# The state chain of a scan half in one step, halves five steps apart and eleven long

## The chip, the cores and the metric

The program runs on one NeuronCore of a Trainium2 chip. The metric is the device time of one execution, in microseconds (us); the median of several runs counts.

## What is computed

Two transformer blocks, one behind the other, with all weights in HBM. The first, one layer over 512 tokens, mixes dilated attention, a gated linear attention (GLA) and block attention. The second, two layers over 512 tokens and 256 context tokens, mixes a Fourier part, attention and a recurrent scan that runs forward and backward. Both scans are chunked forms of the same recurrence. In short:

```python
def step(s, inp):                      # one chunk
    cum = jnp.cumsum(lf, axis=2)       # log forget gates, summed in the chunk
    last = cum[:, :, -1:, :]
    s_new = jnp.exp(last[:, :, 0, :])[..., None] * s + \
        jnp.einsum('bhsd,bhse->bhde', kc * jnp.exp(last - cum), vc)
    o_inter = jnp.einsum('bhtd,bhde->bhte', qc * jnp.exp(cum), s)
    decay = jnp.exp(jnp.where(mask, diff, -jnp.inf))
    att = jnp.einsum('bhtd,bhsd,bhtsd->bhts', qc, kc, decay)
    return s_new, o_inter + jnp.einsum('bhts,bhse->bhte', att, vc)
```

The result is the same whatever the chunk. Every chunk's state needs the state of the chunk before: s_new = decay * s + update.

## The kernel before

The projections and feed-forward products take most of the time: each fp32 product is made of three passes of rounded high and low parts (`gemm_pe`, lines 655 and 658). Between the projections of a layer lie three **scan stages**, one for each layer. I call them stage G (first block, the GLA scan beside causal attention, 245 to 392 us of the trace), stage M (second block, layer 0, 1100.0 to 1260.2) and stage N (layer 1, 2129.5 to 2286.3). Ahead of and behind them lie projections.

In a scan stage every engine runs two programs that the function `branch` interleaves: the scan and "the other", the attention (and in M and N the Fourier part behind it). Each is a generator that yields its position between 0 and 1 after each step; `branch` always takes the one that is behind. So the order of instructions on each engine is fixed when the program is built: it follows from the number of steps of either side, not from times. All engines use the same positions. An engine runs its instructions strictly in this order, and waits at semaphores.

**Attention step** (`att_pe`, `att_act`, `att_dve`, `att_pool`; "step 6" is its number): TensorE makes scores against one block of 128 keys for two heads (line 1052, then a shift, 1064), ScalarE takes exponentials (1234), TensorE multiplies the exponentials of the step before with the values (1085). GpSimd adds exponentials up (1190). At the end of a group of heads come column sums on TensorE (1102), the reciprocal on ScalarE (1241, 1243) and the weighting on VectorE (1161). Scores of two heads fill two banks, so TensorE can begin step s+1 only when the first exponential of step s is done. The products with the values of a new group wait until the reciprocal of the group before last has been begun (`taken`), and the sums of a group wait for the weighting of the group before (`weighted`). Stage M has 32 such steps, 24 with 512 columns and 8 with 256; N has 24; the causal G has 24, and there each score also waits for a maximum that VectorE takes (1141).

**Scan half** (`scan_pe`, `scan_act`, `scan_dve`; n = 0 to 3): M and N have four halves, two of the forward and two of the backward scan; G has one. A half goes through steps k:
- k=0: floor of the gate on VectorE (1356), exponentials and logarithms on ScalarE (1512, 1515, 1520, in layer 1 also 1524)
- k=1: the cumulative sum (1368 or 1370); k=2: differences (1381 to 1386), then the decay and two exponentials on ScalarE (1529 to 1534)
- k=3: q and k scaled (1391, 1393); k=4: differences (1398, 1400), one exponential (1538); k=5: 1405 to 1411, two exponentials (1541, 1544)
- k=6: q and k for the state (1417, 1421); TensorE makes the scores inside the chunks (1605 to 1614)
- k=7: masks (1432); TensorE transposes the keys (1622); ScalarE copies them (`k_tok`, 1549)
- k=8: TensorE makes the **updates** of all chunks (1631) into PS2 and PS3; VectorE begins the **chain**, one instruction for a link (1450)
- k=9: second part of the chain; k=10: TensorE makes the **outputs** (1644 from the scores, 1650 from the states), which wait for the whole chain
- k=11: VectorE copies the outputs out (1462 or 1464)

Half n begins LAG turns behind half n-1, so in one turn step k of a half meets step k-6 of the next:

```python
LAG = 6
SCAN_TICKS = 12
for tick in range(ticks):
    for n in reversed(range(len(hs))):      # VectorE: the later half first
        if 0 <= tick - LAG * n < SCAN_TICKS:
            step(n, tick - LAG * n)
    yield (tick + 1) / (ticks + READ_TICKS)
```

TensorE and ScalarE take the earlier half first. With H halves there are (H-1) * LAG + SCAN_TICKS turns, 30 for four halves and 12 for one, and five more turns that read the result out. A half's chain has 23 links in M and N (24 chunks of 32 tokens), 15 in G.

Of the kernel before, what the change touches and what calls it, by code (L numbers as in the profile page):

```python
# [46 lines left out]
EXP_CAP = 85.0  # L47
SUB = 16
CH = 32
LAG = 6  # L50


COLS = {}
# [83 lines left out]
def blocks_kernel(nc, dram, out_t):  # L137
# [24 lines left out]
    with ExitStack() as ctx:  # L162
# [166 lines left out]
        v_step = sem("dve_step")  # L329
# [999 lines left out]
        def bank(i):  # L1329
            return PS[2 + i // 2][:, 512 * (i % 2):512 * (i % 2) + 512]  # L1330

        SCAN_TICKS = 12
        READ_TICKS = 5

        def scan_ticks(ss):
            n = sum(s.H for s in ss)
            return (n - 1) * LAG + SCAN_TICKS

# [3 lines left out]
        def scan_dve(v, st, ss):  # L1342
            S = lambda n: local(st, n)
# [3 lines left out]
            def step(n, k):  # L1347
                s, u = hs[n]
# [73 lines left out]
                if k == 7:  # L1422
# [6 lines left out]
                    m = masks[:, int(s.back), :].unsqueeze(1).to_broadcast([P, s.n_out, CH])  # L1429
                    for r in range(s.R):  # L1430
# [2 lines left out]
                                                  blocks(bank(r)[:, 0:w], CH)).then_inc(tell.sem, 1)  # L1433
                        if tell is v_step:
                            v_step.up()
                if k in (8, 9):
                    states = blocks(s.room["states"][:], HD)
                    links = list(zip(s.chain, s.chain[1:]))
                    if k == 8:
                        if n >= 1:  # L1440
                            v.wait_ge(S("outputs").sem, S("outputs").at(n))
                        nc.vector.memset(states[:, s.chain[0], :], 0.0).then_inc(v_step.sem, 1)
                        v.wait_ge(v_step.sem, v_step.up())
                        v.wait_ge(S("decay").sem, S("decay").at(n + 1))
                        v.wait_ge(S("updates").sem, S("updates").at(n + 1))
                    m = -(-len(links) // 2)
                    for i in range((k - 8) * m, min(len(links), (k - 7) * m)):
                        a_, b_ = links[i]
                        tell = S("states") if i == len(links) - 1 else v_step
                        nc.vector.scalar_tensor_tensor(states[:, b_, :], states[:, a_, :], s.room[f"decay{n % 2}"][:, a_:a_ + 1],  # L1450
                                                       bank(a_ % 4)[:, a_ // 4 * HD:a_ // 4 * HD + HD], ALU.mult, ALU.add).then_inc(tell.sem, 1)
                        if tell is v_step:
                            v.wait_ge(v_step.sem, v_step.up())
                if k == 11:
                    v.wait_ge(S("outputs").sem, S("outputs").at(n + 1))
                    for w in range(s.R // 2):
                        dst = s.out(u + w)[:, 0:s.own].rearrange("p (t j c) -> p j t c", j=4, c=CH)
                        for j in range(4):
                            tell = S("out") if w == s.R // 2 - 1 and j == 3 else v_step
                            src = blocks(bank(j)[:, w * s.own // 4:(w + 1) * s.own // 4], CH)  # L1460
                            if s.back:
                                nc.vector.tensor_tensor(dst[:, j], src, dst[:, j], ALU.add).then_inc(tell.sem, 1)
                            else:
                                nc.vector.tensor_copy(dst[:, j], src).then_inc(tell.sem, 1)
                            if tell is v_step:
                                v_step.up()
# [7 lines left out]
            s = ss[-1]  # L1474
# [104 lines left out]
        def scan_pe(p, st, ss):  # L1579
            S = lambda n: local(st, n)  # L1580
# [3 lines left out]
            def step(n, k):  # L1584
                s, u = hs[n]
# [38 lines left out]
                if k == 8:  # L1624
# [7 lines left out]
                                              room["k_tok"][rows, P * t + s.dk * r:P * t + s.dk * r + s.dk],  # L1632
                                              s.v(t, s.R * u + r)[rows, :], start=True, stop=True)
                    mm.then_inc(S("updates").sem, 1)
                if k == 10:
                    p.wait_ge(S("states").sem, S("states").at(n + 1))
                    states = blocks(room["states"][:], HD)
                    att, qi = s.att(), s.parity("qi", n)
# [34 lines left out]
            s = ss[-1]  # L1673
# [546 lines left out]
```

## Time and profile before

| | us |
|---|---|
| median of 3 runs | 2752.66 |
| lowest, highest run | 2739.95, 2752.67 |
| profiled execution, its own time | 2748.97 |
| profiled execution, its span | 2746.8 |
| TensorE busy | 2520.5 (92% of the span) |
| VectorE, ScalarE, GpSimd busy | 855.2, 792.6, 782.4 |
| mean granted clock of TensorE | 0.944 |
| stage M, stage N | 160.2, 156.8 |

The time of an execution is a little above the span, which goes from the first to the last instruction. A granted clock of 1.00 is 2.4 GHz, 0.50 is 1.2 GHz. An entry "[5.29 <-DVE s_states L1450]" says that the engine stood idle for 5.29 us before this row, and that what it waited for last was VectorE's line 1450. PE is TensorE, DVE VectorE, ACT ScalarE, POOL GpSimd.

### The profile page before, as it was taken

What the parts mean: (1) busy time and instruction counts of PE and PEld (TensorE: products, weight loads), DVE (VectorE), ACT (ScalarE), POOL (GpSimd) and SP (SyncE); (2) the same over time, 40 slices, a digit from 0 to 9 for tenths busy, and PEclk for the clock granted to TensorE, in tenths of its full rate; (3) what the DMA queues carried; (4) which work ended last, traced back from release to release, by engine and by line L of the source; (5) the groups of instructions that cost most, each with busy time, mean ns of one, the idle gap of its engine ahead of it and who ended that gap; (6) DMA issues with size and microseconds to landing.
All of it is one profiled execution on the core that took longest, in us unless ns stands there. A gap on an engine that the chain in (4) does not pass through costs nothing.

```text
span 2746.8 us, 38017 instructions
## 1 busy us (share of the span) xinstructions
PE 2520.5 (92%) x16714; PEld 1938.7 (71%) x16714; DVE 855.2 (31%) x1287; ACT 792.6 (29%) x1007; POOL 782.4 (28%) x262
## 2 busy tenths in 40 slices
PE   4998788999998899887989999999799877899998
PEld 3876556777776678345878888888568335688886
DVE  3002335442444541762241101102441652411113
ACT  3122233222224421543232112112431533322222
POOL 1232232333432211420222222222221331344442
PEclk9798799999999999998999999999999778999999
DMA  6542013434443110101111111111210102222221
GB/s 179 129 166 71 17 39 127 180 154 182 156 177 122 56 39 1 46 3 62 62 47 62 62 62 63 71 58 48 71 46 9 45 2 78 77 97 103 92 94 60
DMA packets 42952, 220.52 MB, mean 80 GB/s; under 512 B 4072, under 2 KB 12920, under 8 KB 19492
## 3 DMA queue, kind: packets, MB, share of 16 engines
q1 hardware_dynamic: 35624, 200.52, 20.0%
q10 hardware_dynamic: 7164, 17.57, 2.5%
q8 instruction: 132, 2.16, 0.3%
q14 instruction: 32, 0.26, 0.0%
HBM read 212.05 MB, written 6.03 MB: 79 GB/s over the span
## 4 chain that ended last, share of the span: by engine, by line
PE 75%; DVE 6%; ACT 2%; issue 1%; DMA 0%; POOL 0%; ACTq 0%; DVEq 0%; POOLq 0%
PE PS L655 59%; PE PS L658 3%; PE PS L1052 2%; PE PS L1085 2%; DVE s_states L1450 2%; DVE tmp L587 1%; PE PS L716 1%; DVE a_lo L579 1%; PE PS L1650 1%; PE PS L1758 1%; PE PS L1849 1%; PE PS L537 1%; PE PS L1102 1%; PE PS L1064 1%; PE PS L1826 0%
## 5 line engine op out<-in xcount | busy, mean ns | idle before, releaser
L1967 POOL TENSOR_TENSOR w_lo<-raw,w_hi 128x2048 fp32r<-128x2048 f32 (+2 forms) x146 | 648.6, 4442 | 1617.1 <-ACT w_hi L752 1617.1
L655 PE MATMUL PS<-a_hi,w_hi 128*128 128x512 f32 (+1 forms) x2104 | 698.2, 376 | 90.0 <-DVE a_lo L579 58.4
L655 PE MATMUL PS<-a_lo,w_hi 128*128 128x512 f32 (+1 forms) x2104 | 675.8, 366 | 0.0
L655 PE MATMUL PS<-a_hi,w_lo 128*128 128x512 f32 (+1 forms) x2104 | 673.5, 365 | 0.0
L655 PEld LDWEIGHTS PS<-a_hi,w_hi 128*128 128x128 f32 x2104 | 361.1, 191 | 185.6 <-issue 115.7
L655 PEld LDWEIGHTS PS<-a_lo,w_hi 128*128 128x128 f32 x2104 | 362.4, 191 | 65.9 <-issue 0.7
L655 PEld LDWEIGHTS PS<-a_hi,w_lo 128*128 128x128 f32 x2104 | 359.0, 190 | 66.8
L752 ACT ACTIVATE w_hi<-raw 128x2048 fp32r<-128x2048 f32 (+2 forms) x146 | 270.4, 1852 | 373.8 <-PE PS L655 185.3
L655 PE MATMUL PS<-hid_hi,w_hi 128*128 128x512 f32 (+1 forms) x784 | 262.5, 371 | 0.0
L655 PE MATMUL PS<-hid_lo,w_hi 128*128 128x512 f32 (+1 forms) x784 | 259.0, 367 | 0.0
L655 PE MATMUL PS<-hid_hi,w_lo 128*128 128x512 f32 (+1 forms) x784 | 258.5, 366 | 0.0
L866 DVE TENSOR_TENSOR tmp<-PS,sq 128x768 f32<-128x768 f32 (+1 forms) x44 | 36.3, 825 | 486.4 <-PE PS L655 486.4
L1190 POOL TENSOR_TENSOR acc<-acc,pt 128x512 f32<-128x512 f32 (+3 forms) x100 | 119.7, 1197 | 203.2 <-PE PS L1085 152.1
L655 PEld LDWEIGHTS PS<-hid_hi,w_hi 128*128 128x128 f32 x784 | 135.0, 188 | 30.8 <-issue 6.6
L804 ACT ACTIVATE hid_hi<-tmp 128x512 fp32r<-128x512 f32 (+1 forms) x76 | 52.8, 694 | 358.3 <-DVE tmp L866 250.5
L655 PEld LDWEIGHTS PS<-hid_lo,w_hi 128*128 128x128 f32 x784 | 135.6, 188 | 25.4
L655 PEld LDWEIGHTS PS<-hid_hi,w_lo 128*128 128x128 f32 x784 | 134.4, 188 | 25.5
L852 DVE SCALAR_TENSOR_TENSOR x<-PS,mods,x 128x512 f32<-128x512 f32 x64 | 48.1, 751 | 288.3 <-PE PS L655 288.2
L869 DVE TENSOR_TENSOR hid_lo<-tmp,hid_hi 128x512 fp32r<-128x512 f32 (+1 forms) x76 | 99.8, 1313 | 69.3 <-ACT hid_hi L804 69.3
L1052 PE MATMUL PS<-proj 64*128 64x512 f32 (+3 forms) x208 | 100.1, 652 | 17.2 <-ACT acc L1234 13.2
L658 PE MATMUL PS<-w_hi,a_hi 128*128 128x256 f32 (+1 forms) x352 | 103.9, 295 | 4.0 <-POOL w_lo L1967 4.0
L658 PE MATMUL PS<-w_lo,a_hi 128*128 128x256 f32 (+1 forms) x352 | 102.5, 291 | 0.0
(203 smaller groups left out, 2473.8 us busy)
## 6 DMA issues: line engine op xcount, KB each, us to landing
raw<-in_w_ada SPq DMA_DIRECT2D x48, 1024.0 KB, 6.9
raw<-in_w_ff SPq DMA_DIRECT2D x32, 1024.0 KB, 4.7
raw<-in_w_in SPq DMA_DIRECT2D x27, 1024.0 KB, 4.8
raw<-in_w_gate SPq DMA_DIRECT2D x22, 1024.0 KB, 4.7
raw<-in_w_up SPq DMA_DIRECT2D x22, 1024.0 KB, 4.7
raw<-in_w_down SPq DMA_DIRECT2D x16, 1024.0 KB, 4.7
raw<-in_w_out SPq DMA_DIRECT2D x12, 1024.0 KB, 5.8
raw<-in_w_down SPq DMA_DIRECT2D x8, 768.0 KB, 4.3
```

Source lines behind the costliest of these rows:

```text
L655: mm = p.matmul(ps[:, dst], wv[:, k, idx * P:(idx + 1) * P], av[:, k, dst], start=first, stop=last)
L658: mm = p.matmul(ps[:, 0:ncol], av[:, k, idx * P:(idx + 1) * P], wv[:, k, 0:ncol], start=first, stop=last)
L752: nc.scalar.activation(w_hi[:, m % 2, 0:kt, 0:ncol], raw[:, i % 3, 0:kt, 0:ncol], ACT.Copy).then_inc(s_hi.sem, 1)
L804: nc.scalar.activation(hid_hi[:, tile, span(parts)], tmp[:, h % 2, span(parts)], ACT.Copy).then_inc(s_hhi.sem, 1)
L852: nc.vector.scalar_tensor_tensor(dst[:, tile, own], ps[:, src], mods[:, l, o, c:c + 1], dst[:, tile, own], ALU.mult, ALU.add).then_inc(tel ...
L866: nc.vector.tensor_tensor(tmp[:, h % 2, sp_], ps[:, sp_], sq[:, tile % 2, sp_], ALU.mult).then_inc(s_relu.sem, 1)
L869: nc.vector.tensor_tensor(hid_lo[:, tile, sp_], tmp[:, h % 2, sp_], hid_hi[:, tile, sp_].bitcast(F32), ALU.subtract).then_inc(low.sem, 1)
L1052: p.matmul(turned_ps(m)[:, lo:n], hd["k"][:, P * j:P * (j + 1)], hd["q"][:, grp["c0"] + lo:grp["c0"] + n], start=True, stop=False)
L1085: mm = p.matmul(values_ps(plan, g)[hd["rows"], lo:n], hd["v"][j], exps(plan, s, h, lo, n), start=first, stop=last)
L1190: pool.tensor_tensor(total_, total_, pt[:, s % 2, h, lo:n], ALU.add).then_inc(S("added").sem, 1)
L1450: nc.vector.scalar_tensor_tensor(states[:, b_, :], states[:, a_, :], s.room[f"decay{n % 2}"][:, a_:a_ + 1], bank(a_ % 4)[:, a_ // 4 * HD:a ...
L1967: pool.tensor_tensor(w_lo[:, m % 2, 0:kt, 0:ncol], src, w_hi[:, m % 2, 0:kt, 0:ncol].bitcast(F32), ALU.subtract).then_inc(s_lo.sem, 1)
```

## The change

LAG becomes 5 and SCAN_TICKS 11. The whole chain is made in step k=8; the outputs move from k=10 to k=9 and the copies from k=11 to k=10. The number of turns falls from 30 to 26 in M and N (35 to 31 with the reading), and from 12 to 11 in G (17 to 16), so each turn is a larger share of the stage and the places of all scan steps among the attention steps shift. In one turn step k of a half now meets step k-5 of the next half, and step 10 of a half, step 5 of the next and step 0 of the one after meet.

```diff
-LAG = 6
+LAG = 5
...
-        SCAN_TICKS = 12
+        SCAN_TICKS = 11
...
-                if k in (8, 9):
+                if k == 8:
                     states = blocks(s.room["states"][:], HD)
                     links = list(zip(s.chain, s.chain[1:]))
...
-                    m = -(-len(links) // 2)
-                    for i in range((k - 8) * m, min(len(links), (k - 7) * m)):
-                        a_, b_ = links[i]
+                    for i, (a_, b_) in enumerate(links):
                         tell = S("states") if i == len(links) - 1 else v_step
                         nc.vector.scalar_tensor_tensor(states[:, b_, :], states[:, a_, :], s.room[f"decay{n % 2}"][:, a_:a_ + 1],
                                                        bank(a_ % 4)[:, a_ // 4 * HD:a_ // 4 * HD + HD], ALU.mult, ALU.add).then_inc(tell.sem, 1)
                         if tell is v_step:
                             v.wait_ge(v_step.sem, v_step.up())
-                if k == 11:
+                if k == 10:
                     v.wait_ge(S("outputs").sem, S("outputs").at(n + 1))
...
-                if k == 10:
+                if k == 9:
                     p.wait_ge(S("states").sem, S("states").at(n + 1))
```

Three lines are gone, so a line number of the scan above 1441 is three or so lower in the changed kernel.

ScalarE in stage N, where half 0's step 5 meets half 1's step 0. Before (E is the exponential's output, pt the attention's exponentials, acc those of a group's first step):

```order
602 L1234 ACTIVATE pt<-PS 128x512 x2
603 L1541 ACTIVATE s_E_113<-s_X 128x768
604 L1544 ACTIVATE s_E_114<-s_d 128x768
605 L1234 ACTIVATE pt<-PS 128x512 x2
606 L1512 ACTIVATE proj<-proj 128x768
607 L1515 ACTIVATE s_lf_pad<-proj,small 128x768
608 L1520 ACTIVATE s_F<-s_lf_pad 128x768
609 L1524 ACTIVATE s_lf_pad<-s_F,lbs 128x768
610 L1234 ACTIVATE acc_82<-PS 128x512 x2
```

and now:

```order
599 L1234 ACTIVATE pt<-PS 128x512 x2
600 L1538 ACTIVATE s_E_113<-s_X 128x768
601 L1541 ACTIVATE s_E_114<-s_d 128x768
602 L1509 ACTIVATE proj<-proj 128x768
603 L1512 ACTIVATE s_lf_pad<-proj,small 128x768
604 L1517 ACTIVATE s_F<-s_lf_pad 128x768
605 L1521 ACTIVATE s_lf_pad<-s_F,lbs 128x768
606 L1234 ACTIVATE pt<-PS 128x512 x2
607 L1234 ACTIVATE acc_82<-PS 128x512 x2
```

The exponentials of attention step 5 stood between the two groups of the scan and stand behind both now.

TensorE in stage M, half 1, from the column sums of step 18 to the outputs (the updates stood ahead of step 18 before, with four steps of one row 1052 to 1085 each between transposes and outputs). Before:

```order
4098 L1102 MATMUL PS<-acc_82,ones 64x512 x2
4099 L1102 MATMUL PS<-pt,ones 64x512 x2
4100 L1052 MATMUL PS<-proj,k_swap 128x512
4101 L1052 MATMUL PS<-proj 128x512
4102 L1064 MATMUL PS<-shift,ones_r 128x512 x2
4103 L1085 MATMUL PS<-acc_82,tok_57 64x512 x2
4104 L1052 MATMUL PS<-proj,k_swap 128x512
4105 L1052 MATMUL PS<-proj 128x512
4106 L1064 MATMUL PS<-shift,ones_r 128x512 x2
4107 L1085 MATMUL PS<-pt,tok_57 64x512 x2
4108 L1644 MATMUL PS<-s_att_128,tok_57 64x32 x48
```

and now:

```order
4097 L1102 MATMUL PS<-acc_82,ones 64x512 x2
4098 L1102 MATMUL PS<-pt,ones 64x512 x2
4099 L1628 MATMUL PS<-tok_57,s_k_tok 64x64 x48
4100 L1052 MATMUL PS<-proj,k_swap 128x512
4101 L1052 MATMUL PS<-proj 128x512
4102 L1064 MATMUL PS<-shift,ones_r 128x512 x2
4103 L1085 MATMUL PS<-acc_82,tok_57 64x512 x2
4104 L1641 MATMUL PS<-s_att_128,tok_57 64x32 x48
```

The updates (1628) have moved behind the sums, and one attention step instead of three lies between them and the outputs. In M the halves have 2, 1, 2 and 0 steps there (3, 3, 3 and 0 before), in N 1, 1, 1 and 0 (2, 2, 2 and 0 before).

VectorE in stage M, half 2. Before:

```order
493 L1442 MEMSET s_states 128x64
494 L1450 SCALAR_TENSOR_TENSOR s_states<-s_states,s_decay_126,PS 128x64 x12
495 L1161 TENSOR_TENSOR proj<-PS,inverse 128x512
496 L1391 TENSOR_TENSOR s_qb<-proj,s_E_113 128x768
497 L1393 TENSOR_TENSOR s_kb<-proj,s_E_114 128x768
498 L1450 SCALAR_TENSOR_TENSOR s_states<-s_states,s_decay_126,PS 128x64 x11
```

and now:

```order
490 L1391 TENSOR_TENSOR s_qb<-proj,s_E_113 128x768
491 L1393 TENSOR_TENSOR s_kb<-proj,s_E_114 128x768
492 L1441 MEMSET s_states 128x64
493 L1447 SCALAR_TENSOR_TENSOR s_states<-s_states,s_decay_126,PS 128x64 x23
494 L1161 TENSOR_TENSOR proj<-PS,inverse 128x512
```

Step 3 of the next half (1391, 1393) has come ahead of the chain, and the weighting (1161) has moved from behind 12 links to behind all 23.

## Rows read from the trace of the kernel before

**Rows 1.** Windows: busy time by engine and granted clock, stages M and N

```profile
core 0: us, PE busy (x) PEld busy (x) DVE busy (x) ACT busy (x) POOL busy (x), PEclk, DMA share, GB/s
1100.00:1260.20 160.20, 134.52 (x2520) 68.04 (x2520) 103.05 (x188) 68.86 (x121) 48.72 (x32) 0.87 0.06 21
2129.50:2286.30 156.80, 122.09 (x1832) 56.07 (x1832) 88.04 (x184) 64.27 (x101) 44.08 (x32) 0.76 0.06 21
```

**Rows 2.** What TensorE waited for, longest first, in stage N

```profile
PE PS L1644 <- DVE s_states L1450: 23.9, 4, 8.0
```

**Rows 3.** TensorE in time order (start, duration, what, [idle before]), N, half 0

```profile
2155.24 0.73 PE L1614 MATMUL PS<-s_qb,s_kb 64*32 64x32 f32 x62
2156.43 0.69 PE L1052 MATMUL PS<-proj 64*128 64x512 f32 x1
2160.64 0.87 PE L1622 MATMUL PS<-ident,s_ko 128*128 128x128 f32 x6
2164.01 1.25 PE L1631 MATMUL PS<-tok,s_k_tok 32*64 32x64 f32 x96
2176.35 1.18 PE L1644 MATMUL PS<-s_att,tok 32*64 32x32 f32 x64 [5.29 <-DVE s_states L1450]
```

**Rows 4.** VectorE in order of time, stage N, half 0

```profile
2165.97 3.76 DVE L1450 SCALAR_TENSOR_TENSOR s_states<-s_states,s_decay,PS 128x64 f32<-128x64 f32 x12
2169.77 0.69 DVE L1161 TENSOR_TENSOR proj<-PS,inverse 128x512 f32<-128x512 f32 x1
2171.20 1.74 DVE L1393 TENSOR_TENSOR s_kb<-proj,s_E 128x512 f32<-128x512 f32 x1
2172.86 3.43 DVE L1450 SCALAR_TENSOR_TENSOR s_states<-s_states,s_decay,PS 128x64 f32<-128x64 f32 x11
```

**Rows 5.** ScalarE in order of time, stage N, halves 0 and 1

```profile
2154.51 0.84 ACT L1544 ACTIVATE s_E<-s_d 128x768 f32<-128x768 f32 x1 [1.08 <-DVE s_d L1411]
2155.26 1.07 ACT L1234 ACTIVATE pt<-PS 128x512 f32<-128x512 f32 x2
2156.21 0.84 ACT L1512 ACTIVATE proj<-proj 128x768 f32<-128x768 f32 x1
2157.09 0.94 ACT L1515 ACTIVATE s_lf_pad<-proj,small 128x768 f32<-128x768 f32 x1
2158.06 0.84 ACT L1520 ACTIVATE s_F<-s_lf_pad 128x768 f32<-128x768 f32 x1
2158.93 1.03 ACT L1524 ACTIVATE s_lf_pad<-s_F,lbs 128x768 f32<-128x768 f32 x1
2161.55 0.81 ACT L1549 ACTIVATE s_k_tok<-PS 128x768 f32<-128x768 f32 x1 [0.61 <-PE PS L1622]
```

**Rows 6.** TensorE in order of time, stage M, half 1

```profile
1168.78 0.88 PE L1622 MATMUL PS<-ident,s_ko 128*128 128x128 f32 x6
1172.09 1.25 PE L1631 MATMUL PS<-tok,s_k_tok 32*64 32x64 f32 x96
1183.06 1.17 PE L1644 MATMUL PS<-s_att,tok 32*64 32x32 f32 x96
```

**Rows 7.** TensorE in order of time, stage M, half 2

```profile
1210.10 0.65 PE L1085 MATMUL PS<-acc,tok 128*64 128x256 f32 x4 [0.53 <-ACT inverse L1241]
1216.62 1.12 PE L1102 MATMUL PS<-acc,ones 128*64 128x256 f32 x4 [3.15 <-DVE proj L1161]
```

**Rows 8.** Windows: the 11 us behind half 0's wait in stage N

```profile
2176.30:2187.30 11.00, 10.95 (x142) 6.12 (x142) 5.08 (x12) 3.39 (x5) 2.54 (x2) 0.50 0.01 1
```

**Rows 9.** TensorE in time order: products with the states, M, halves 0 and 3

```profile
1153.41 2.99 PE L1650 MATMUL PS<-s_qi,s_states 64*64 64x32 f32 x96
...
1254.97 5.33 PE L1650 MATMUL PS<-s_qi,s_states 64*64 64x32 f32 x96
```

**Rows 10.** VectorE in order of time, stage G

```profile
323.44 2.50 DVE L1450 SCALAR_TENSOR_TENSOR s_states<-s_states,s_decay,PS 128x64 f32<-128x64 f32 x8 [2.19 <-PE PS L1631]
```

**Rows 11.** TensorE in order of time, stage G

```profile
326.32 0.39 PE L1039 MATMUL PS<-a_lo,a_hi 64*128 64x256 f32 x1 [0.16 <-DVE small L1141]
```

More of the change, by code:

```diff
@@ L1435, in step @@
                             v_step.up()
-                if k in (8, 9):
+                if k == 8:
                     states = blocks(s.room["states"][:], HD)
                     links = list(zip(s.chain, s.chain[1:]))
[L1439 to L1445, printed above, removed]
-                    m = -(-len(links) // 2)
-                    for i in range((k - 8) * m, min(len(links), (k - 7) * m)):
-                        a_, b_ = links[i]
+                    if n >= 1:
+                        v.wait_ge(S("outputs").sem, S("outputs").at(n))
+                    nc.vector.memset(states[:, s.chain[0], :], 0.0).then_inc(v_step.sem, 1)
+                    v.wait_ge(v_step.sem, v_step.up())
+                    v.wait_ge(S("decay").sem, S("decay").at(n + 1))
+                    v.wait_ge(S("updates").sem, S("updates").at(n + 1))
+                    for i, (a_, b_) in enumerate(links):
                         tell = S("states") if i == len(links) - 1 else v_step
```

## The prediction

> **What bounds the kernel now.** I read the windows of the stages first, then the waits of TensorE, then the timelines around the state chain. TensorE is the engine that sets the end nearly everywhere; in the scan stages it is not full. In stage M it is busy 134.5 of 160.2 us at a mean granted clock of 0.87, in stage N 122.1 of 156.8 us at 0.76 [rows 1]. So a stage gets longer when TensorE waits more or when its clock stays low longer; its work is the same before and after. In stage N the largest wait is four times the same one: the outputs of a half (line 1644) wait for the state chain on VectorE, 23.9 us in all, 8.0 the longest [rows 2]. Rows 3 and 4 show one of these. The updates end at 2164.01 + 1.25 = 2165.26. Then TensorE has two attention steps, about 2.9 us each, and stands 5.29 us until 2176.35 [rows 3]. VectorE meanwhile runs chain (3.76), the attention's weighting (0.69), the next half's step 3 (about 2.4 us between 2170.46 and 2172.86) and chain (3.43) [rows 4]. These 11.1 us are what the change wants to shorten.
>
> **What moves.** Nothing is removed: the 23 links of a half stay 23 links, 3.76 + 3.43 = 7.2 us [rows 4]. What changes is which work lies between two waits.
> (a) VectorE: the chain runs in one piece behind the updates, and the next half's step 3 comes ahead of it.
> (b) TensorE: between updates and outputs lie now one or two attention steps where two or three were.
> (c) ScalarE: a half's step 5 and the next half's step 0 now fall in one turn, and so do step 7 and the next half's step 2. The exponentials of the attention step are queued behind the pair. TensorE can begin the next attention step without them, but not the one after.
>
> **Stage N, cost of each part.**
> Outputs' wait. Path behind the updates: about 0.15 to the first link, 7.2 of chain, 0.1 to TensorE, together 7.45, less one step of 2.9: 4.6 in place of 5.29, a gain of 0.7 in halves 0 to 2. In half 3 the weighting (0.69) no longer lies between the two pieces: 0.7 too. Together -2.8.
> Given back: step 3 of the next half must end before the chain starts. It needs that half's two exponentials, which now stand behind k_tok. Counted from the transposes: k_tok ends at 2162.36 - 2160.64 = 1.7 [rows 3, 5], two exponentials of 0.84 make 3.4, step 3 makes 5.8. The updates end 4.6 behind the transposes where one step lies between [rows 3]. So 1.2 each for halves 0 and 1: +2.4. In half 2 two steps lie between, and there the attention's reciprocal stands behind the same two exponentials: +1.6. Net of the outputs' part: +1.2.
> The pair on ScalarE. Half 0's last exponential ends at 2155.35; half 1's four operations take 2156.21 to 2159.96, 3.75 us [rows 5]. Before, attention step 5 had its exponentials between the two (2155.26, 1.07 for two). Now they come after: first one ready at 2155.35 + 3.75 + 0.55 = 2159.65. TensorE is done with step 5 at 2155.24 and used to go on with scores and step 6 [rows 3]; now step 6 comes first and waits: 4.4 us. Once only, since in the later halves the products with the states (4.8 us) and the scores lie where they cover the pair.
> The clock. Behind the wait of 5.29 the granted clock is 0.50 for 11 us, the 1.2 GHz level [rows 8]. All but 0.05 us of them is busy, so at most 5.5 us is lost. A new wait of 4.4 costs between 0 and 5.5; I take 4.5, since it is nearest in length to this row.
> Stage N: 1.2 + 4.4 + 4.5 = +10.1.
>
> **Stage M.** Here three attention steps lay between updates and outputs and the wait was near nothing.
> Half 0: the reciprocal for step 7 stands behind the pair, about 1.8 us of waiting; two steps with sums almost cover the chain, 0.5. +2.3.
> Half 1: the pair is half 1's two exponentials (1.6) and three operations (2.65). With the first attention exponential it takes 4.8 us against one step of 2.8: 2.0. The exponentials behind k_tok: 0.5. Between updates and outputs one step of 2.7 is left where steps and sums filled 1172.09 + 1.25 to 1183.06 without a gap [rows 6]: 7.45 - 2.7 = 4.8. After it the clock: the 96 products on the states took 2.99 at the full clock and 5.33 at the low one [rows 9], +2.3, those on the scores +0.4, one attention step +1.8: 4.6, with bounds 0 and 5.5. Together +11.9.
> Half 2: the reciprocal waits for two more exponentials, +1.9 on the 0.53 there [rows 7]. The column sums wait for the weighting, which stood behind the first half of the chain (3.15 us [rows 7]) and stands behind all of it now: +3.4, the second piece's length [rows 4]. Clock +1.0. Together +6.3.
> Half 3: the last attention step moves into the wait for k_tok (0.9) and 0.35 of weighting leaves the chain: -1.3.
> Stage M: 2.3 + 11.9 + 6.3 - 1.3 = +19.2.
>
> **Stage G.** One half of 15 links: 8 take 2.50 [rows 10], so 4.7 in one piece. The attention there needs a maximum from VectorE for each score; one waits 0.16 now [rows 11]. It would find VectorE in the chain until 0.7 + 4.7 + 0.6 = 6.0 behind the updates, with 2.5 us of work for TensorE: 3.4. Some of it may be won back where the transposes stand one attention step later. +2, bounds 0 and 3.4.
>
> **Sum.** 10.1 + 19.2 + 2.0 = +31.3 on the profiled execution's 2748.97: 2780. The runs' median is 2752.66, 3.7 above that execution, and one run had 2739.95, so the base is known to about that.
>
> The price of a link deserves a second look: 3.43 / 11 = 0.312 us for 64 columns. [...]
>
> **Rivals.**
> 1. *The cover holds.* The pairs on ScalarE may cost nothing if its exponentials run early enough, and new waits may leave the clock alone. Then 10.6 us of pair terms and 10.1 of clock go, and +10.6 is left: 2760, within 0.5%. For it: ScalarE is busy only 69 of 160 us [rows 1]. Against: the pair is 5.4 us in one piece and TensorE is one step ahead at most. 0.20.
> 2. *Faster: the outputs' waits in stage N get short enough for the clock to stay up.* The three of 5.29 become 4.6 by the chain's path. The point from which it decides: if 4.6 us of idling leaves TensorE at 2.4 GHz and 5.29 doesn't, stage N wins 3 x 5 us of low clock, and 2.8 of waiting; with the pairs covered too, 2749 - 18 = 2731. Against: 3.15 us of waiting [rows 7] stands in a stretch whose work is already slower. 0.06.
> 3. *Every pair stalls.* If the products and scores don't cover the pairs in halves 1 and 2 either, 4.4 + 4.5 come on top perhaps twice more: 2798. 0.12.
> 4. *Nothing moves:* excluded by the order of the rows on all three engines.
>
> **How the numbers follow.** A measurement of this kernel can tell 0.5% (13.8 us) from no change. Forecast as summed: 0.62, its own range 2765 (clock terms at 0, small terms low) to 2793 (5.5 of clock behind four new waits). Rival 1: 0.20, rival 2: 0.06, rival 3: 0.12. So slower by over 0.5% (above 2766.4) 0.74, within 0.5% 0.20, faster 0.06. The range leaves out rival 2 and the low part of rival 1, and takes in rival 3: 2756 to 2800.
>
> **What would show it.** Right: in stage N one new wait of 4 to 5 us on ScalarE's exponentials near attention step 6, with the clock at 0.5 behind it; outputs' waits of 4 to 6 us; in stage M a wait of about 5 us at half 1's outputs and one of about 6.5 us for the weighting in half 2; stage M near 179 us, stage N near 167. Wrong: stage M under 170 us, no wait on exponentials, or the loss outside the three scan stages.

## The result, and the profile after

The changed kernel takes 2796.57 us (median of 4 runs, 2794.3 to 2799.63), the kernel before 2752.66 in the same comparison: ratio 1.0174, 95% interval 1.0147 to 1.0201. The medians are 43.9 us apart; the ratio stands for 48 us. The forecast was 2780, slower, with 2756 to 2800 as its range. Sign and range held; the size did not: 31 us were forecast, 44 to 48 came.

The profiled execution has 2794.3 us, span 2792.5. The windows of stages M and N, whole, as in [rows 1] (columns: from:to, length, busy time by engine, granted clock, DMA share, GB/s):

```profile
1094.94:1291.03 196.09, 157.77 (x2520) 77.48 (x2521) 97.78 (x188) 68.51 (x121) 47.15 (x32) 0.73 0.05 17
2160.31:2331.40 171.09, 134.60 (x1832) 58.91 (x1832) 81.97 (x184) 64.25 (x101) 43.48 (x32) 0.68 0.05 19
```

M went from 160.2 to 196.1 us (179 forecast), N from 156.8 to 171.1 (167 forecast). TensorE has the same instructions and is busy 23 and 12.5 us longer, at a lower clock. What TensorE waited for, in M and then in N (total us, times, longest):

```profile
PE PS L1641 <- DVE s_states L1447: 14.4, 3, 7.4
PE PS L1102 <- DVE proj L1161: 5.3, 1, 5.3
PE PS L1085 <- ACT inverse L1241: 3.7, 2, 2.1
PE PS L1052 <- ACT pt L1234: 1.8, 2, 1.4
...
PE PS L1641 <- DVE s_states L1447: 22.1, 4, 7.4
PE PS L1052 <- ACT pt L1234: 3.0, 1, 3.0
PE PS L1085 <- ACT inverse L1241: 1.6, 1, 1.6
```

In N the outputs' waits fell from 23.9 [rows 2] to 22.1, and one wait for the exponentials came new, as forecast. In M the waits for the states are 2.07, 4.94 and 7.44 us (halves 0, 1 and 3). The forecast rows in TensorE's timeline, M and then N:

```profile
1157.29 1.17 PE L1641 MATMUL PS<-s_att,tok 32*64 32x32 f32 x96 [2.07 <-DVE s_states L1447]
1232.94 0.65 PE L1085 MATMUL PS<-acc,tok 128*64 128x256 f32 x4 [2.11 <-ACT inverse L1241]
1242.96 1.12 PE L1102 MATMUL PS<-acc,ones 128*64 128x256 f32 x4 [5.32 <-DVE proj L1161]
2190.89 1.22 PE L1052 MATMUL PS<-proj 64*128 64x512 f32 x1 [3.02 <-ACT pt L1234]
2213.98 1.18 PE L1641 MATMUL PS<-s_att,tok 32*64 32x32 f32 x64 [4.98 <-DVE s_states L1447]
```

And the whole chain of a half on VectorE, 7.25 us for 23 links, the 3.76 + 3.43 of [rows 4] in one piece:

```profile
2206.68 7.25 DVE L1447 SCALAR_TENSOR_TENSOR s_states<-s_states,s_decay,PS 128x64 f32<-128x64 f32 x23
```

So the waits are those that were forecast. The clock is not. The first of these windows lies just ahead of the 2.07 us wait and the second behind it, the third behind a wait of 1.42 us, the fourth behind the 4.94 us wait:

```profile
1144.50:1154.50 10.00, 10.00 (x133) 3.97 (x134) 7.00 (x18) 5.53 (x10) 4.96 (x4) 1.00 0.01 2
1157.29:1168.49 11.20, 11.20 (x204) 7.04 (x206) 5.37 (x12) 4.69 (x8) 0.85 (x1) 0.59 0.01 3
1183.40:1191.86 8.46, 8.45 (x124) 3.34 (x124) 3.52 (x11) 3.36 (x7) 0.00 (x0) 1.00 0.01 2
1196.80:1214.00 17.20, 17.20 (x220) 9.73 (x222) 4.91 (x11) 4.92 (x8) 4.70 (x4) 0.60 0.01 2
```

TensorE was busy without a gap at the full clock, stood idle for 2.07 us, and then had a mean clock of 0.59 for 11.2 us: with the two levels 1.0 and 0.5 that is 2 x 0.41 x 11.2 = 9.2 us at 1.2 GHz, a loss of 4.6 us behind a wait of 2.07. The forecast had put waiting, and no clock, on this place. The third row begins behind a wait of 1.42 us, and there the clock stayed at 1.00. The second profile (after_again, below) has the same three waits with 0.58, 1.00 and a low clock behind them.

In half 2 the forecast had "Clock +1.0". From the column sums, which waited for the weighting, to the end of the half's outputs, before (behind 3.15 us) and after (behind 5.32 us):

```profile
1216.62:1227.37 10.75, 10.75 (x230) 7.19 (x230) 7.84 (x19) 3.65 (x9) 0.00 (x0) 0.86 0.01 2
1242.96:1254.46 11.50, 11.50 (x212) 8.60 (x212) 3.20 (x6) 2.19 (x5) 0.00 (x0) 0.50 0.00 1
```

At 0.50 the 11.50 us lose half their length, 5.75 us; at 0.86 the 10.75 us lose 1.5. So the clock cost over 4 us more here than before, against the 1.0 forecast; the second profiles of both kernels have 0.50 and 0.85.

### The profile page after: what moved, and what is told of

It reads as the page before. It is cut to its first block, busy times and chain, and to the rows that moved or that the text cites. A ratio compares the mean times of both kernels' runs of the same rounds, so it can differ in the third digit from the quotient of the medians.

```text
span 2792.5 us, 38011 instructions
## 1 busy us (share of the span) xinstructions
PE 2553.1 (91%) x16714; PEld 1950.7 (70%) x16714; DVE 843.9 (30%) x1287; ACT 792.4 (28%) x1007; POOL 779.6 (28%) x262
## 4 chain that ended last, share of the span: by engine, by line
PE 76%; DVE 6%; ACT 3%; issue 1%; POOL 0%; DMA 0%; ACTq 0%; DVEq 0%; POOLq 0%
PE PS L655 58%; PE PS L658 2%; PE PS L1052 2%; PE PS L1085 2%; DVE s_states L1447 2%; DVE tmp L587 1%; PE PS L716 1%; DVE a_lo L579 1%; PE PS L1647 1%; PE PS L1755 1%; PE PS L1846 1%; PE PS L1064 1%; PE PS L1102 1%; PE PS L537 1%; PE PS L1747 1%
## 5 line engine op out<-in xcount | busy, mean ns | idle before, releaser
L1052 PE MATMUL PS<-proj 64*128 64x512 f32 (+3 forms) x208 | 114.4, 726 | 21.4 <-ACT acc L1234 15.0
```

What stands on the lines that cost most here:

```text
L1052: p.matmul(turned_ps(m)[:, lo:n], hd["k"][:, P * j:P * (j + 1)], hd["q"][:, grp["c0"] + lo:grp["c0"] + n], start=True, stop=False)
```

## The experiments

All ratios are against runs of the kernel before on the same chip. "Spacing" is LAG, "length" is SCAN_TICKS. First the results together, ordered by what they share:

| kernel | spacing, length, chain | median us | ratio (95%) |
|---|---|---|---|
| before_again | 6, 12, split | 2750.29 | 1.0012 (0.9988 to 1.0035) |
| lag6_one12 | 6, 12, whole | 2746.93 | 0.9978 (0.9951 to 1.0005) |
| lag6_one | 6, 11, whole | 2766.90 | 1.0058 (1.0035 to 1.0082) |
| lag5_split | 5, 12, split | 2779.57 | 1.0097 (1.0066 to 1.0128) |
| lag5_one12 | 5, 12, whole | 2779.00 | 1.0078 (1.0049 to 1.0107) |
| after_again | 5, 11, whole | 2794.76 | 1.0176 (1.0133 to 1.0218) |
| lag7_one12 | 7, 12, whole | 2789.59 | 1.0138 (1.0114 to 1.0163) |
| act_k0_late | 5, 11, whole | 2795.54 | 1.0181 (1.0139 to 1.0224) |
| before_pair | 6, 12, split | 2755.07 | 1.0016 (0.9995 to 1.0037) |
| before_nochain | 6, 12, none | 2697.33 | 0.9801 (0.9758 to 0.9844) |
| pair_nochain | 6, 12, none | 2704.99 | 0.9838 (0.9804 to 0.9873) |
| after_nochain | 5, 11, none | 2719.23 | 0.9882 (0.9855 to 0.9910) |
| start_before | 6, 12, split, filled | 2756.66 | 1.0006 (0.9984 to 1.0027) |
| warm_before | 6, 12, split, filled | 2736.91 | 0.9940 (0.9916 to 0.9964) |
| warm_12 | 6, 12, whole, filled | 2738.96 | 0.9953 (0.9923 to 0.9983) |
| warm_all | 6, 12, whole, filled | 2746.78 | 0.9977 (0.9956 to 0.9998) |
| warm_after | 5, 11, whole, filled | 2788.28 | 1.0129 (1.0098 to 1.0161) |
| after_fill | 5, 11, whole, filled | 2778.44 | 1.0120 (1.0094 to 1.0147) |

### Both kernels once more

> The changed kernel unaltered, for a second profile. In the first, stage M's part up to the first outputs took 62.9 us against 52.9 before, with the same instructions and nearly the same waits, at a granted clock of 0.78 against 0.90. Theory A1 (how long the clock stays low behind the start wait of 4.3 us differs from execution to execution): that part may come out between 52 and 63 us in this profile. Theory A2 (it follows from the order of the work): 62 to 63 us again. The ratio to the kernel before stays 1.015 to 1.020.

> The kernel before unaltered, for a second profile. A1: stage M's part up to the first outputs (52.9 us, clock 0.90) may come out as long as 61 us, and stage M up to 10 us longer than 160.8 us without any edit; A2: 52 to 54 us again. Ratio 0.998 to 1.002.

The windows from the end of the attention's start wait (4.3 us in M, 5.2 in N) to the end of the last outputs, M and N, of the first and second profile before, then of the first and second after:

```profile
1107.11:1260.24 153.13, 132.97 (x2515) 67.60 (x2515) 97.45 (x182) 64.31 (x116) 48.72 (x32) 0.88 0.05 20
2136.49:2286.32 149.83, 120.48 (x1826) 55.55 (x1826) 84.47 (x180) 58.68 (x95) 44.08 (x32) 0.75 0.05 19
```

```profile
1103.60:1263.68 160.08, 139.82 (x2515) 69.13 (x2515) 94.61 (x182) 64.27 (x116) 46.64 (x32) 0.82 0.05 19
2139.73:2293.56 153.83, 124.65 (x1826) 56.39 (x1826) 83.42 (x180) 58.76 (x95) 44.21 (x32) 0.72 0.05 18
```

```profile
1102.09:1291.03 188.94, 156.14 (x2514) 77.00 (x2515) 92.14 (x182) 63.96 (x116) 47.15 (x32) 0.73 0.04 15
2167.27:2331.41 164.14, 132.98 (x1827) 58.43 (x1827) 78.42 (x180) 58.67 (x95) 43.48 (x32) 0.68 0.05 18
```

```profile
1116.51:1299.29 182.78, 150.58 (x2515) 76.60 (x2515) 94.15 (x182) 63.91 (x116) 47.70 (x32) 0.77 0.04 16
2174.66:2333.56 158.90, 123.61 (x1827) 56.34 (x1827) 81.56 (x180) 58.98 (x95) 43.68 (x32) 0.75 0.05 18
```

A1 holds in its main point: the same kernel's stage M differs by 7 us from profile to profile, all of it busy time at another clock (idle is 20.2 and 20.3). Only the place guessed was wrong: the kernel before's part up to the first outputs stayed near 53 us, and most of the difference (40.2 against 45.3 us) lies between the outputs of half 1 and those of half 2. A single pair of profiles therefore overstates or understates the clock. The means of the two are used from here; taken pair by pair, the added busy time is 10.8 to 23.2 us in M and -1.0 to 12.5 us in N. After less before: M +29.3 (busy +17.0, idle +12.3), N +9.7 (busy +5.7, idle +4.0), ahead of M +3.9, the rest +0.5. Together 43.4, which is the difference of the mean spans (2793.55 - 2750.25).

### The change taken apart: spacing, length, chain

lag6_one, against the changed kernel:

```diff
-LAG = 5
+LAG = 6
```

> Eleven steps with the whole chain in step 8, but the halves six steps apart again, so that no two halves meet on ScalarE in one tick. Theory A (the chain's path of 7.45 us now has one attention step for cover instead of two or three, and each wait that this makes on TensorE lowers its granted clock, which costs more than the wait): the time is that of the changed kernel, 2790 to 2800 us, with waits of 4.5 to 5 us in stage N. Theory B (the five-step spacing does it: two halves' exponentials meet on ScalarE): the time goes back to 2750 to 2760 us.

lag5_split, against the kernel before:

```diff
-LAG = 6
+LAG = 5
```

> Only the spacing is changed, six steps to five; the chain stays in two pieces over twelve steps. Theory A: the outputs keep two or three attention steps of cover, so no wait is added; the time is 2750 to 2762 us, and the granted clock of stages M and N stays near 0.87 and 0.76. Theory B: the waits for ScalarE's pt are there (2 to 4 us each) and the clock falls behind them, 2775 to 2800 us.

lag6_one12, against the changed kernel, first the copies, then the outputs (lag5_one12 is the same with LAG = 5):

```diff
-LAG = 5
+LAG = 6
-        SCAN_TICKS = 11
+        SCAN_TICKS = 12
-                if k == 10:
+                if k == 11:
...
-                if k == 9:
+                if k == 10:
```

> Six steps apart and twelve long as before, only the chain goes whole into step 8, the outputs stay in step 10. Theory A: the waits in front of the outputs in stage N fall from 5.3 us to 7.45 - 5.8 = 1.6 us, the clock falls less behind them, 2730 to 2745 us. Theory C (the whole chain on VectorE holds up what stands behind it, above all the weighting of an attention group, and that is where the loss comes from): new waits for VectorE of 3 to 6 us, 2760 to 2785 us.

> Five steps apart, twelve long, whole chain in step 8, outputs in step 10: the missing corner between the split chain at five apart (1.010) and the changed kernel (1.018). If the spacing and the outputs' step add up as they did at six apart (0.998 with the outputs in step 10, 1.006 in step 9): 1.006 to 1.011. If at five apart the whole chain itself is what costs, through VectorE's later weighting and copies: 1.013 to 1.018.

Neither A nor B alone: lag6_one lies between the two forecasts, lag5_split in B's range, lag6_one12 just above A's, and lag5_one12 where it was expected if the parts add up. The six kernels (these four, before and after_again) add up. Whole in place of split chain: -0.19% at five apart, -0.22% at six, which is within the uncertainty. Outputs and copies one step earlier, a half eleven steps long: +0.80% at six apart, +0.98% at five (22 and 27 us). Spacing five in place of six: +0.97%, +1.00% and +1.18% (27 to 32 us). So the change is two losses of similar size, and the piece it is named for, the chain in one step, is the one whose cost can't be told from nothing.

The waits show how. TensorE in N of lag6_one12, and then of lag6_one:

```profile
PE PS L1641 <- DVE s_states L1447: 14.0, 4, 7.4
```

```profile
PE PS L1641 <- DVE s_states L1447: 22.8, 4, 7.4
```

With one more attention step under the chain the waits of halves 0 to 2 are 2.2 us each (1.6 expected) instead of 4.94 to 5.51. Theory C's wait is seen in M: the weighting behind the whole chain is waited for 6.5 us (3.15 in [rows 7]); its loss is not seen in the time. In lag5_split a conflict comes that the changed kernel does not have, since at five apart and twelve long the copies of a half share a turn with the next half's scores. M, and then N:

```profile
PE PS L1614 <- DVE proj L1464: 7.4, 1, 7.4
...
PE PS L1085 <- ACT inverse L1241: 4.7, 3, 1.6
PE PS L1052 <- ACT pt L1234: 3.0, 1, 3.0
PE PS L1614 <- DVE proj L1464: 2.6, 1, 2.6
```

So its 1.0097 is not the price of the spacing alone; the pair lag6_one and after_again, without that conflict, gives 1.18%.

lag7_one12, against lag6_one12:

```diff
-LAG = 6
+LAG = 7
```

> Seven steps apart, twelve long, whole chain in step 8, outputs in step 10 (at six apart this measured 0.998). Theory A and D (spacing sets how much attention lies beside each half, and so the waits): the three meetings of step 6, 7 with the next half's step 0 are apart, the waits of half 0 to 2 stay at 2.2 us, but the scan ends three steps later, so that its last half has less attention beside it: 0.995 to 1.003.

A miss: 1.0138. In M:

```profile
PE PS L1085 <- ACT inverse L1241: 10.7, 4, 6.3
PE PS L1052 <- ACT pt L1234: 8.1, 3, 7.5
```

ScalarE has work in steps 0, 2, 4, 5 and 7 of a half. At six apart no two of these fall in one turn. At five, 5 meets 0 and 7 meets 2; at seven, 7 meets 0. But it is not this meeting that makes the two longest waits, of 7.51 and 6.33 us. VectorE and ScalarE ahead of the 7.51:

```profile
1133.21 7.25 DVE L1447 SCALAR_TENSOR_TENSOR s_states<-s_states,s_decay,PS 128x64 f32<-128x64 f32 x23
1142.88 0.84 ACT L1529 ACTIVATE s_E<-s_d 128x768 f32<-128x768 f32 x1 [7.90 <-DVE s_d L1386]
```

At seven apart step 8 of a half shares its turn with step 1 of the next, so the next half's step 2 (its differences, up to line 1386) stands behind the whole chain on VectorE. ScalarE stands 7.90 us for it, and the attention's exponentials are queued behind; the 6.33 comes the same way, behind 7.06 us on ScalarE. At six apart step 2 shares the turn of step 8 and VectorE takes the later half first, so it stands ahead of the chain. Wider is no better than closer: what stands behind the long chain decides here.

### Is it the meeting on ScalarE?

act_k0_late, against the changed kernel, on ScalarE:

```diff
-                if k == 0:
+                if k == (0 if n == 0 else 1):
```

> The changed kernel, but ScalarE issues step 0 of halves 1 to 3 one tick later, where the half ahead has nothing for it: no two halves meet on ScalarE. Theory B (about half of the loss is these meetings, each a wait for pt of 1.4 to 3 us and the clock behind it): those waits go and 8 to 15 us come back, ratio 1.011 to 1.014. Theory A alone (the outputs' waits do it): within 4 us of the changed kernel, ratio 1.016 to 1.019; a wait of VectorE for the logarithm, 1.5 us each, could take its place.

Nothing came back (1.0181 against 1.0176), but the test is not clean. In M and N the later step made VectorE late, and TensorE waited for that instead, and N still has a first attention wait of 3.0 us:

```profile
PE PS L1619 <- DVE s_ko L1421: 4.0, 1, 4.0
...
PE PS L1052 <- ACT pt L1234: 3.7, 3, 3.0
PE PS L1628 <- DVE s_att L1432: 2.6, 2, 1.5
```

That wait is not the meeting's: its exponentials came 19.6 us behind the end of the start wait, against 23.6 and 23.2 in the two profiles of the changed kernel, but TensorE had the higher clock and was there sooner. For the same reason the meeting's wait is 3.02 us in one profile of the changed kernel and 6.09 in the other: ScalarE is ready at the same time, and TensorE arrives 20.6 or 17.2 us behind the start wait.

The other way round is cleaner: make the meeting of 5 and 0 where there was none.

before_pair, against the kernel before, on ScalarE; VectorE makes the floor of halves 1 to 3 one turn earlier too:

```diff
-                if k == 0:
+                if k == (0 if n == 0 else -1):
...
-                    if 0 <= tick - LAG * n < SCAN_TICKS:
+                    if -1 <= tick - LAG * n < SCAN_TICKS:
```

> The kernel before, six apart, twelve long, split chain; only step 0 of halves 1 to 3 (the floor on VectorE, the exponentials and logarithms on ScalarE) is issued one tick earlier, so that it meets step 5 of the half ahead on ScalarE as it does at five apart. Theory B (the meeting itself delays pt and the reciprocals, and the clock falls behind those waits): waits for pt of 1.5 to 3 us as in the changed kernel, 10 to 20 us slower, ratio 1.004 to 1.007. Theory D (the meeting is harmless, it is the spacing of five that packs more work of two halves beside fewer attention steps): 0.998 to 1.002.

> The same meeting with the chain left out (all the states cleared and only the last link issued, so the recurrence is not computed): nothing but the meeting differs from the kernel that measured 0.9801. Theory B: it comes near the changed kernel without its chain, 0.985 to 0.989. Theory D: 0.978 to 0.982.

```profile
PE PS L1647 <- DVE s_states L1450: 23.9, 4, 8.0
...
PE PS L1052 <- ACT pt L1234: 4.9, 1, 4.9
```

The forecast wait is there in N, 4.9 us (4.4 by the forecast's sum), once. The time is 1.0016 (0.9995 to 1.0037): at most 10 us, below the 1.004 of theory B and as D has it. Without the chain the two medians give 0.37% (10 us), between B and D, but each ratio is known to some 0.4% and their difference can't be told from nothing. So the meeting of 5 and 0 by itself carries at most about 10 of the 27 to 32 us. The rest lies with what else five apart does: 7 meeting 2, the reciprocals behind both, and fewer attention steps for each half. These were not separated.

### The chain left out

before_nochain (after_nochain and pair_nochain in the same way):

```diff
-                            nc.vector.memset(states[:, s.chain[0], :], 0.0)
+                            nc.vector.memset(s.room["states"][:], 0.0)
-                    m = -(-len(links) // 2)
-                    for i in range((k - 8) * m, min(len(links), (k - 7) * m)):
+                    links = links[-1:] if k == 8 else []
+                    for i in range(len(links)):
```

> The kernel before with the chain left out: VectorE clears all the states ahead of the updates and issues the last link alone, so the recurrence over the chunks is not computed. Outputs no longer wait for 7.45 us of links. Theory A: the waits for the states in stages M and N (8.1 and 23.9 us) go and with them the low clock behind them, 45 to 60 us in all: ratio 0.978 to 0.984. If only the waits count: 30 us or less, 0.989 and above.

> The changed kernel with the chain left out in the same way. It takes from both kernels what the exposed chain costs and leaves the spacing of five and the eleven steps. Theory A (the exposed chain with its clock is nearly all of the 45 us): after_nochain lies within 12 us of before_nochain. Theory B (the meetings on ScalarE and the reciprocals they hold up are at least half): it lies 20 us or more above before_nochain.

The windows behind the start wait, M and N, before and after without the chain:

```profile
1114.25:1261.11 146.86, 136.08 (x2515) 66.72 (x2515) 76.35 (x94) 64.15 (x116) 47.72 (x32) 0.86 0.05 20
2138.27:2249.37 111.10, 105.23 (x1827) 46.84 (x1827) 69.45 (x92) 58.55 (x95) 44.03 (x32) 0.88 0.07 26
```

```profile
1099.17:1260.70 161.53, 145.67 (x2514) 68.47 (x2514) 72.60 (x94) 63.46 (x116) 45.86 (x32) 0.81 0.05 19
2126.68:2251.56 124.88, 112.50 (x1827) 48.76 (x1827) 64.69 (x92) 58.53 (x95) 44.61 (x32) 0.83 0.06 23
```

The exposed chain costs the kernel before 54 us, as theory A had it, in N the clock as well as the wait: N lost 23.4 us of idling and 17.3 of busy time against the means above, M 9.4 of idling and 0.3 of busy time. Between the medians of the two kernels 22 us stay without any chain, but their ratios leave 8 to 36 us, so that neither A's limit of 12 nor B's 20 is settled. In the windows above M has 5.1 us more idling and 9.6 more busy time, N 6.5 and 7.3; yet the two profiled executions differ by 1.8 us only, since what lies outside these windows was longer in that of before_nochain, one of its slowest runs. A cost of five apart and eleven long without a chain is there, of the size of the spacing's; it was not separated between these two.

### The waits filled

In these kernels TensorE gets extra matmuls on the identity ahead of a wait, into a bank of their own. The kernel's own work stays as it is. A filling waits until its bank is free, though, and other waits can move: in N warm_after waits 1.83 and 1.29 us for exponentials where the changed kernel does not.

The core of warm_after, against the changed kernel (g is the group of heads that the attention is in; the bank is the one that its sums will take):

```diff
                 if k == 9:
+                    count = 0 if s.gla else ((0, 30, 0, 0), (30, 30, 30, 0))[s.l][n]
...
+                        for _ in range(count):
+                            p.matmul(PS[1][:, 512 * ((g + 1) % 2):512 * ((g + 1) % 2) + P], ident[:], ident[:], start=True, stop=True)
                     p.wait_ge(S("states").sem, S("states").at(n + 1))
```

> The changed kernel, with 30 extra matmuls of 128 columns on TensorE (about 4.4 us at the full clock, their result is not read) just ahead of the outputs' wait of half 1 in stage M and of halves 0, 1 and 2 in stage N: the wait is filled, not shortened. Theory A (the clock that falls behind a wait is most of the loss): the granted clock behind these four places stays up and 12 to 25 us come back, 2772 to 2785 us. If the waits themselves were the loss: nothing comes back, 2794 to 2800 us, or some us more where the filling runs longer than the wait.

> The kernel before, waits filled with extra matmuls whose result is not read (30 in the attention's start wait of stages M and N, 30 ahead of the outputs of halves 0 to 2 in stage N, 48 ahead of those of half 3 in both). No wait is made shorter. Theory A: the clock stays up behind them, 20 to 35 us come back, ratio 0.987 to 0.993. If the clock were incidental: 0.998 to 1.004.

> The changed kernel with its waits filled by extra matmuls whose result is not read: 30 in the attention's start wait of stages M and N, 20 in the wait for pt of half 0 in stage N (3.0 us), 30 ahead of the outputs of halves 0 to 2 in stage N, 48 ahead of those of half 3 in both. Theory A: the granted clock in stage N is over 0.93, stage N behind its start wait takes 139 to 146 us instead of 159 to 164, as short as the kernel before filled in the same way (139.5), and the time is 2760 to 2775 us, ratio 1.004 to 1.009. If the clock were incidental: 1.015 to 1.020.

> The kernel before with only the attention's start wait filled (30 extra matmuls of 128 columns, result not read) in stages M and N, 4.3 and 5.2 us. Theory A: behind it stage M's first part runs at a clock of 1.00 instead of 0.89 to 0.93 and is 4 to 6 us shorter, the same in N, ratio 0.996 to 0.999. Otherwise 1.000 to 1.003.

> Whole chain in step 8, outputs in step 10, six steps apart (the kernel that measured 0.998), with 30 extra matmuls of 128 columns in the start wait of the attention in stages M and N (4.3 and 5.2 us) and 14 in front of each outputs' wait of halves 0 to 2 in stage N (2.2 us). Theory A: the clock stays up behind them, 10 to 20 us less than without: 2725 to 2738 us, ratio 0.990 to 0.995. If waits as such are the cost: ratio 0.998 to 1.002.

> The kernel that measured 0.995 (whole chain in step 8, outputs in step 10, six apart, start waits and the outputs' waits of halves 0 to 2 of stage N filled), with 48 more filling matmuls ahead of the outputs of half 3 in both stages (7.44 us each, behind which the products with the states took 6.8 and 4.7 us at the low clock). Theory A: these take about half, and the Fourier part behind them starts at the full clock, 5 to 12 us less: ratio 0.991 to 0.994.

My estimate of 4.4 us for 30 was too low; half 0's in N of warm_before took 6.96 at the full clock, and the outputs followed at once:

```profile
2179.47 6.96 PE L1651 MATMUL PS<-ident 128*128 128x128 f32 x60
2186.36 0.86 PE L1665 MATMUL PS<-s_att,tok 32*64 32x32 f32 x64
2187.16 2.05 PE L1671 MATMUL PS<-s_qi,s_states 64*64 64x32 f32 x64
```

So each filling of 30 runs up to 2 us past a wait of 5 and still pays. The products with the states take 2.05 us here and 3.62 in the kernel before behind each of its waits for the states in N. The windows of N behind the start wait, or behind its filling, of warm_after, warm_before and after_fill:

```profile
2184.63:2334.83 150.20, 130.84 (x2007) 70.68 (x2007) 81.60 (x180) 58.98 (x95) 44.01 (x32) 0.86 0.05 19
```

```profile
2148.12:2279.01 130.89, 126.48 (x2104) 76.08 (x2103) 82.40 (x177) 58.06 (x94) 44.17 (x32) 0.99 0.05 17
```

```profile
2169.44:2316.47 147.03, 137.91 (x2143) 82.08 (x2142) 78.31 (x177) 58.47 (x94) 43.42 (x32) 0.94 0.04 16
```

Behind the start wait, stage N of the changed kernel comes down from 161.5 (mean) to 150.2 with three fillings, at 0.86 instead of 0.68 to 0.75, and to 147.0 at 0.94 with all; that of the kernel before from 151.8 to 130.9, at 0.99. (The 139.5 in an expectation above is a window that takes in the filling of the start wait.) The time follows: 0.994 for the kernel before, 1.0129 for warm_after (a little outside the range expected on the slow side), 1.012 for after_fill (N a little above the 139 to 146 that were expected, and the total above its range too). In warm_after the filling in M failed: it had to wait 6.5 us itself, for the weighting that frees the bank, and stage M got 6 us longer. Filling takes 13 to 17 us from either kernel and leaves their distance about as it was: it shows that a wait costs its clock, not that these waits are the difference.

start_before, expected at 0.996 to 0.999, came out at 1.0006 (0.9984 to 1.0027), which settles nothing. Its first part of M ran at the full clock, as expected, and later parts, which it does not touch, at 0.79 and 0.59:

```profile
1111.61:1152.70 41.09, 39.90 (x431) 15.01 (x430) 31.70 (x45) 22.92 (x39) 26.00 (x16) 1.00 0.10 40
1152.70:1193.60 40.90, 38.82 (x577) 16.35 (x577) 24.37 (x49) 18.02 (x30) 16.03 (x11) 0.79 0.01 2
1236.50:1272.70 36.20, 24.93 (x635) 17.11 (x633) 11.92 (x36) 6.54 (x15) 0.00 (x0) 0.59 0.01 2
```

4 us won at one place are within what the other places vary by, and the filling itself ran 1.8 to 2.7 us too long in each stage. The second of these rows also shows a fall of the clock that no long wait explains. TensorE had been at 1.00 and waited 0.51 us for the states; with one more gap of 0.50 us among the products with them came a mean clock of 0.57 for 7.9 us:

```profile
1152.72 1.17 PE L1647 MATMUL PS<-s_att,tok 32*64 32x32 f32 x96 [0.51 <-DVE s_states L1453]
1156.13:1164.00 7.87, 7.87 (x56) 3.21 (x55) 3.54 (x9) 2.55 (x4) 1.30 (x2) 0.57 0.01 2
```

warm_12 came out at the edge of its range; its three fillings in N each waited 2.8 us for the weighting first, so they did not close the gap ahead of the outputs. warm_all was expected below warm_12 and came out above it (0.9977 against 0.9953, not clearly apart): its 48 matmuls take 48 x 0.232 = 11.1 us against waits of 7.44. warm_before and warm_12 are 0.5 to 0.6% faster than the kernel before. Fillings as long as the wait, into a bank that is free, were not tried.

## Why the prediction was right or wrong

- **Sign and waits: right.** One new wait for the exponentials in N near attention step 6 (4.4 forecast; 3.02 and, in the second profile, 6.09), outputs' waits in N of 4.7 to 5.0 (4.6 forecast), half 1's outputs in M 4.94 (4.8), the weighting 5.32 (6.5), the chain 7.25 (7.2).
- **Waits: right in sum too.** Stage M 13.6 forecast, 12.3 measured as idling; stage N 5.6 and 4.0.
- **Clock in stage N: not contradicted.** 4.5 forecast, 5.7 measured as added busy time in the mean, but -1.0 to 12.5 pair by pair.
- **Clock in stage M: the step that failed.** The forecast charged "4.6, with bounds 0 and 5.5" in half 1 and "Clock +1.0" in half 2, 5.6 together; measured 17.0 in the mean, and 10.8 even in the mildest pair of profiles. Two places are shown, in both profiles: behind half 0's outputs' wait, put down at 0.5 of waiting and no clock, 2.07 us of waiting cost 4.6 of clock; behind the weighting's wait of half 2, put down at 1.0, the clock cost over 4 more than before. In half 0 and in half 3 the clock had no term at all. In the kernel before, the part of M from half 0's outputs to half 1's ran its whole 30.8 us at 1.00, with 0.32 us ahead of it as the only wait; after, no part of M did. Waits of a microsecond or more (without the start wait) went from 5 to 10 in M and from 6 to 8 in N; three of them in M and two in N, in both kernels, are gaps for which the profile names no engine. That the number of waits makes the rest of the 17.0 is my reading; the 0.51 us of start_before shows that a count of long waits does not hold all of it.
- **Stage G and what lies ahead of M:** +2 forecast, +3.9 measured, but the two profiles of the changed kernel differ there by 14.4 us; so this term is neither shown nor refuted.
- Sum: 31.3 forecast; 12.3 + 4.0 + 5.7 + 17.0 + 3.9 and 0.5 of rest make 43.4. Of the 12 us missing, 11.4 are stage M's clock.
- **By part of the change:** terms that hang on five apart (pairs, step 3 given back, reciprocals, N's clock) summed to 19.1, those of chain and outputs to 12.2. Measured 27 to 32 and 16 (lag6_one) to 22 (after_again over lag5_split): each about one and a half times as dear. That the clock is the reason in both is likely and not shown for each.
- **Rivals:** 1 (the cover holds) fell: waits and clock are there. 2 (faster) fell: behind 4.98 us the clock was 0.74 as far as the next outputs. Even lag6_one12 with waits of 2.2 us had 0.73 to 0.88 in N's halves behind them, and gained only 0.2%. 3 (every pair stalls, 2798) came nearest in time, but by another way: in M the waits for the exponentials behind the pairs are 0.37 and 1.42 us.
- **The range** held by luck: rival 3 had been taken in, and its stalls did not come. The forecast's own range, to 2793, did not hold. Its upper end, 5.5 of clock behind four new waits in place of the 10.1, adds 31.3 - 10.1 + 22 = 43.2 us, close to what came.
- **A small slip:** 2.3 + 0.4 + 1.8 for the clock in half 1 make 4.5, not 4.6.

## What to carry to other kernels

Where one engine sets the end and its clock follows its idling, give every new wait a clock term, the short ones too: here 4.6 us of clock came behind a wait of 2.07, as much as had been forecast behind one of 4.8. Shortening a pipeline of interleaved steps is not free even if each step keeps its work: write down in which steps each engine has work and what each spacing puts behind the long serial piece (at seven apart the next half's differences stood behind the chain), and leave that piece its cover. Take two profiles of each kernel before reading a clock difference of a few microseconds from one.

## What was not expected of the hardware

- Behind the same wait the low clock lasts for different times. After the 4.3 us start wait of M, half 0's part up to the outputs took 45.2 us in the kernel before and 55.2 in the changed one in their first profiles, with 3.3 us more of waiting (1.57 for the reciprocal, the rest at the outputs); in the second, 46.9 and 50.0. lag6_one12 had 53.3 without either wait. Nothing in these rows says which it will be.
- A wait of 2.07 us lowered the granted clock of an engine that had been busy without a gap (1.00 to a mean of 0.59 over 11.2 us), while one of 1.42 us in the same stage left it at 1.00. In start_before it fell behind 0.51 us and a gap of 0.50.
- Matmuls whose result nobody reads made the kernel before 0.6% faster.
